# Spreading one-hot groups over the whole U stage, and loading a V group's tiles in four pieces between gathers

## What is computed

```python
def block(xb):                                   # for each token
    q = (xb @ w_q).reshape(p, HEADS, 2, 64)
    sc = einsum('phcd,hcnd->phcn', q, sub_keys)
    top_s, top_i = top_k(sc, 16)                 # of 128 keys, for both halves
    cand_s = top_s[..., 0, :, None] + top_s[..., 1, None, :]
    best_s, best_pos = top_k(cand_s, 16)         # 16 of 256 pairs
    idx = ...                                    # 8 heads * 16 of 16384 experts
    g = softmax(best_s)
    act = gelu(einsum('phkd,pd->phk', expert_u[idx], xb))
    return einsum('phk,phkd->pd', g * act, expert_v[idx])
```

## Time and profile before

| what | us |
|---|---|
| median of 3 runs | 2368.6 |
| the profiled execution | 2364.9 |
| its span | 2363.6 |
| PE busy | 2249.3 (95%) |
| DVE busy | 1616.6 (68%) |
| POOL busy | 1062.2 (45%) |
| ACT busy | 850.0 (36%) |

### The profile page before, as it was taken

How to read it: one execution, slowest core, us unless ns; L and a number is a source line. 1 busy time by engine, 2 the same in 40 slices (tenths; PEclk the granted TensorE clock), 3 DMA queues, 4 the chain that set the end, 5 groups by cost and what they waited for, 6 DMA issues and landing times.

```text
span 2363.6 us, 29994 instructions
## 1 busy us (share of the span) xinstructions
PE 2249.3 (95%) x11272; PEld 2031.7 (86%) x11272; DVE 1616.6 (68%) x3044; ACT 850.0 (36%) x1317; POOL 1062.2 (45%) x666
## 2 busy tenths in 40 slices
PE   6999999999889999899999989999999989999998
PEld 3777889998889999889899988998887778888887
DVE  6774699999996525878787878865756556444333
ACT  4433433333334333233333323354345533322221
POOL 1444207788888873545454645543332331111100
PEclk9999999999899999999999999999999999999999
DMA  7647747667668866999999999942424252333332
GB/s 291 196 139 248 218 126 183 171 154 172 151 150 201 210 169 202 338 367 353 374 343 368 338 366 331 347 152 85 122 74 118 74 178 89 102 95 98 103 98 76
DMA packets 205464, 470.89 MB, mean 199 GB/s; under 512 B 50364, under 2 KB 105788, under 8 KB 200768
## 3 DMA queue, kind: packets, MB, share of 16 engines
q1 hardware_dynamic: 136408, 316.76, 41.2%
q0 software_dynamic: 68912, 152.21, 21.0%
HBM read 403.68 MB, written 61.28 MB: 197 GB/s over the span
## 4 chain that ended last, share of the span: by engine, by line
PE 34%; DMA 11%; DVE 11%; POOL 3%; issue 2%; ACT 1%; DVEq 0%; ACTq 0%
PE bank L568 8%; PE bank L572 8%; PE bank L569 8%; DMA row_over<-in_rows_u,row_at 2%; DMA rows<-in_rows_v,row_at 2%; DVE own L2116 2%; DMA scaled<-in_rows_v,row_at 2%; DVE weights_lo L1654 2%; DMA square<-in_rows_u,row_at 2%; DMA rows<-in_rows_u,row_at 2%; DVE hidden L2077 1%; PE bank_stat L947 1%; PE bank_stat L948 1%; PE bank_stat L952 1%; DVE rows L2110 1%
## 5 line engine op out<-in xcount | busy, mean ns | idle before, releaser
L568 PE MATMUL bank<-h_lo,weights_hi 128*128 128x416 f32 (+1 forms) x2148 | 796.0, 371 | 10.2 <-DVE gates L2330 3.8
L569 PE MATMUL bank<-h_hi,weights_hi 128*128 128x416 f32 (+1 forms) x2148 | 791.1, 368 | 0.0
L1131 ACT ACTIVATE weights_hi<-weights_raw 128x1024 fp32r<-128x1024 f32 (+1 forms) x411 | 431.5, 1050 | 311.9 <-DMA weights_raw<-in_expert_v 176.8
L1654 DVE TENSOR_TENSOR weights_lo<-weights_raw,weights_hi 128x1024 fp32r<-128x1024 f32 x351 | 443.1, 1263 | 146.9 <-ACT weights_hi L1131 144.2
L2508 POOL DMA_INDIRECT expert_coefs<-square x256 | 444.3, 1735 | 157.7 <-issue 78.8
L572 PE MATMUL bank<-h_hi,weights_lo 128*128 128x416 f32 (+1 forms) x2148 | 482.8, 366 | 15.8 <-DVE weights_lo L1654 15.4
L568 PEld LDWEIGHTS bank<-h_lo,weights_hi 128*128 128x128 f32 x2148 | 411.1, 191 | 46.0 <-DVE gates L2330 3.9
L572 PEld LDWEIGHTS bank<-h_hi,weights_lo 128*128 128x128 f32 x2148 | 403.7, 189 | 51.5 <-DVE weights_lo L1654 21.2
L569 PEld LDWEIGHTS bank<-h_hi,weights_hi 128*128 128x128 f32 x2148 | 410.9, 191 | 30.7 <-issue 0.2
L2455 POOL TENSOR_TENSOR weights_lo<-weights_raw,weights_hi 128x1024 fp32r<-128x1024 f32 x60 | 147.9, 2471 | 220.6 <-ACT weights_hi L1131 220.6
L1342 ACT ACTIVATE hidden<-bank 128x416 f32<-128x416 f32 x128 | 66.2, 518 | 347.2 <-PE bank L572 331.6
(11 more groups left out here) (471 smaller groups left out, 3530.1 us busy)
## 6 DMA issues: line engine op xcount, KB each, us to landing
weights_raw<-in_expert_u SPq DMA_DIRECT2D x128, 512.0 KB
weights_raw<-in_expert_v SPq DMA_DIRECT2D x128, 512.0 KB
weight<-expert_coefs POOLq DMA_DIRECT2D x16, 1664.0 KB, 11.0
hidden_store<-hidden SPq DMA_DIRECT2D x28, 832.0 KB
hidden<-hidden_store POOLq DMA_DIRECT2D x14, 1664.0 KB, 15.8
ada_raw<-in_w_ada SPq DMA_DIRECT2D x34, 512.0 KB, 6.5
expert_coefs<-zeros SPq DMA_DIRECT2D x32, 512.0 KB, 6.4
weights_raw<-in_w_ffn_gate SPq DMA_DIRECT2D x22, 512.0 KB
```

The lines of the kernel that those rows point to most:

```text
L568: M.matmul(bank[:, 0:width], hi[:, c:c + P], m_lo[k][:, 0:width], start=start and i == 0, stop=False)
L569: M.matmul(bank[:, 0:width], hi[:, c:c + P], m_hi[k][:, 0:width], start=False, stop=False)
L1131: S.activation(w_hi[n % SPLIT][:, 0:w], w_raw[n % RAW][:, 0:w], ACT.Copy).then_inc(*hi_done.inc(n))
L1654: V.tensor_tensor(w_lo[n % SPLIT][:, 0:w], w_raw[n % RAW][:, 0:w], w_hi[n % SPLIT][:, 0:w].bitcast(F32), ALU.subtract).then_inc(*lo_dve.in ...
```

## The change

Two edits that don't depend on each other.

The first moves work inside the U stage. The routing steps of block 3 stand at every third step from j = 46 to j = 97, where they stood at every second from 46 to 80. The 32 quads of block 2 stand from j = 48 to 98 (before: one at each step from 48 to 79), and the 8 quads of block 3 from 100 to 112 (before: 83 to 97). The own tokens are copied at j = 113 (before: 98). No instruction is added or taken away.

The second cuts each `load_group` into four DMAs (two halves of the coefficients, two halves of the hidden values) and issues them after the gathers number 4, 6, 8 and 10 of the group, counted from 0, where both whole DMAs stood after gather 4. The wait for the hidden values of `mix_tile` becomes two: at tile 0 for the first half, at tile 4 for the second. The first two groups are loaded ahead of the gathers as before, in more pieces.

```diff
         for tb in range(1, TB):
-            step = 2 if tb == TB - 1 else 1
+            step = 3 if tb == TB - 1 else 1
             ROUTED_AT.append([ROUTED_AT[-1][-1] + 1 + step * n for n in range(ROUTE_STEPS)])
...
-            room = min(n_quads * TB // 2, QUADS, AHEAD * GROUP - 2 - first)
+            room = (ROUTED_AT[TB - 1][-1] + 3 if tb < TB - 1 else AHEAD * GROUP - 6) - first
...
                 if n == 0:
-                    V.wait_ge(*weight_landed[g % 2][g])
-                    if g < KEPT:
-                        V.wait_ge(*hidden_landed[g % 2][g])
+                    V.wait_ge(*weight_landed[g % 2][g, 1])
+                if n in (0, HALF) and g < KEPT:
+                    V.wait_ge(*hidden_landed[g % 2][g, n])
...
                     if i >= 2:
                         G.wait_ge(*dve["mix_lo", MIX_ORDER[i - 2], GROUP - 1])
-                    G.dma_start(weight[g % 2][:].rearrange("p s j t -> p (s j t)"),
-                                coefs[g].rearrange("p s j t -> p (s j t)")).then_inc(*weight_landed[g % 2].inc(g))
+                    half = DT // TOK // 2
+                    for part in range(2):
+                        yield G.dma_start(weight[g % 2][:, part * half:(part + 1) * half].rearrange("p s j t -> p (s j t)"),
+                                          coefs[g, :, part * half:(part + 1) * half].rearrange("p s j t -> p (s j t)")) \
+                            .then_inc(*weight_landed[g % 2].inc((g, part)))
                     if g < KEPT:
                         G.wait_ge(*hidden_stored[g % 2][g, HALF])
-                        G.dma_start(hidden[g % 2][:], hidden_store[g]).then_inc(*hidden_landed[g % 2].inc(g))
-
-            load_group(0)
+                        for n in (0, HALF):
+                            yield G.dma_start(hidden[g % 2][:, n:n + HALF, :], hidden_store[g, :, n:n + HALF, :]) \
+                                .then_inc(*hidden_landed[g % 2].inc((g, n)))
...
+                pieces = load_group(i + 2)
                 for n, q in enumerate(steps_here):
                     load_rows(q)
-                    if n == ROWS - 1:
-                        load_group(i + 2)
-                if len(steps_here) < ROWS:
-                    load_group(i + 2)
+                    if n >= ROWS - 1 and (n - ROWS + 1) % 2 == 0:
+                        next(pieces, None)
+                for _ in pieces:
+                    pass
```

More of the change, by code:

```diff
@@ L2520, in load_group @@
                         G.wait_ge(*dve["mix_lo", MIX_ORDER[i - 2], GROUP - 1])
-                    G.dma_start(weight[g % 2][:].rearrange("p s j t -> p (s j t)"),
-                                coefs[g].rearrange("p s j t -> p (s j t)")).then_inc(*weight_landed[g % 2].inc(g))
+                    half = DT // TOK // 2
[3 more added lines that the diff above has]
+                            .then_inc(*weight_landed[g % 2].inc((g, part)))
                     if g < KEPT:
                         G.wait_ge(*hidden_stored[g % 2][g, HALF])
-                        G.dma_start(hidden[g % 2][:], hidden_store[g]).then_inc(*hidden_landed[g % 2].inc(g))
-            load_group(0)
+                        for n in (0, HALF):
+                            yield G.dma_start(hidden[g % 2][:, n:n + HALF, :], hidden_store[g, :, n:n + HALF, :]) \
+                                .then_inc(*hidden_landed[g % 2].inc((g, n)))
+            for _ in load_group(0):
+                pass
             G.dma_start(position[:], a["positions"]).then_inc(*position_landed.inc("position"))
-            load_group(1)
+            for _ in load_group(1):
+                pass
             def load_rows(q):
```

## The result

The changed kernel takes 2302.3 us (median of four runs, 2296.5 to 2305.8) against 2368.6: a ratio of 0.9716, with an interval of 0.969 to 0.9741. It is 66 us faster; the forecast was 40. The profiled execution took 2305.8 us with a span of 2304.5, 59.1 us under the span of before. The part behind the last group, which no edit of this document touches, took 807.9 to 814.3 us in the fourteen traces: that is how much two executions differ there alone.

A forecast was written before the change was run, and what follows sets the result against it. VectorE was taken to bound the U stage's middle, TensorE its end, with GpSimd's scatters alongside, and VectorE with one late gather the V stage. 2364.9 - 2 - 38 = 2324.9 us, as a median 2328; range 2312 to 2360.

The forecast's parts named there:

- The U stage: U stage, first edit: TensorE sets the pace, so u119 comes about 30 us earlier, near 878 us.
- Where that gain goes: End of U stage: nowhere; TensorE stands still some 30 us because the first mixing waits for coefficients behind the last scatter.
- The hand-over's own shift: Scatters' end before the first mixing: -2 us taken, with -6 and +21 us kept as ends.
- The 2 us for calls beside an idle VectorE: Last 20 us or so of scatters: about 11 calls at 1.54 us rather than 1.735, 2 us less.
- The V stage: V stage, second edit: VectorE's stop for the late gather goes; 14 periods shorten by 2.7 us each, -38 us.
- the allowance for queueing: V stage: gathers and weight blocks queue now and then near the 418 GB/s ceiling, so 37.1 us a period (382 GB/s).
- the sign of being right: V stage in the profile after: the loads' spacing is 36.5 to 37.5 us.
- the best case: V stage: all 14 passes with a load fall from 39.8 to 35.8 us, -56 us.
- 8.5 against 13.0: V stage: a gather behind a piece lands in 8.5 us, where five buffers in flight allow 13.0 us.
- the two favourable ends: The scatters' end at -6 us and the V stage's gain at -56 us.
- The rule against small DMAs: Skill's rule of DMAs of at least 1 MiB: 30 more would cost an estimated 60 us in series; expected to cost little.
- the wrong one of these two rules: Scatters: the skill's inference that two-input instructions don't lock GpSimd out would make the -2 us term 0.

The follow-up runs named there:

- the two cut kernels: The last 32 of 256 scatters left out: the changed kernel so cut took 2281.1 us (0.9649), the kernel before so cut 2359.9 us (0.9977).
- the run that fills the pause by order: Changed kernel with the splits and gelus of u120 to u127 put ahead of group 14's mixing on VectorE and ScalarE: 2307.7 us, 0.9751.
- the run with the cut-down chain: Changed kernel with table steps done before the coefficients, seven row steps spread over the V stage, mixing in pairs beside the last four splits: 2282.7 us, 0.9644.

## Why the prediction came out short

Its mechanisms held in the main, and two terms of its sum were too small.

- **The U stage.** Right: u119 at 878.45 us (forecast: near 878, with 4 us allowed for small stalls; that it fits to the microsecond is luck), steps of 4.5 to 5.0 us nearly throughout, the clock at 1.00.
- **Where that gain goes.** Right: a pause up to the first mixing. That it hangs on the scatters is shown by the two cut kernels. The pause costs clock (0.79 and 0.88 in the two stretches, 0.70 from 905 to 915 us), and mostly under the cover of VectorE's chain, as was said: the chain of waits runs through VectorE and the one gather from 904.2 to 941.6 us. Not covered is a second dip behind the stop at 939 us: the last eight matmuls of group 14's first product take 3.14 us (944.04) where they take 1.67 at the full clock (922.42, above).
- **The hand-over's own shift: -2 us taken, 8 to 9 measured.** This is the first mis-sized term. The last scatter ended 5.8 us earlier, where -6 had been named as the end of the range and -2 taken. The 2 us for calls beside an idle VectorE were right (30.2 us for 32.5); what failed is the step that left the calls ahead of these at their old mean, though quads now run beside them; the 20 just before gained 0.5 to 5 us. And one part was missed: the coefficients land 6.8 us after GpSimd begins to issue them (897.41 to 904.2), where it had been 9.1. In those 9.1 us the DMA queues also moved 0.52 MB of other data, a block of weights; in the 6.8 us none. The second edit alone (6.9, none) and the run that fills the pause by order (8.5, 0.53 MB) fit this, so it goes with the weight loads and not with TensorE's pause as such; the first edit alone, whose load is whole, takes 7.3 with none. The chain of waits has the last 6.2 of these, from the issue of the second piece:

```profile
898.02 6.17 DMA weight<-expert_coefs
```

- **The V stage: -38 us taken, 51 to 52 measured.** The second and larger one. VectorE's waits for gathers fell from 103 us to 23 (forecast: under 30) and TensorE is what is late next, as written. The step that failed is the allowance for queueing: 37.1 us a period was taken for a data rate near its ceiling, and TensorE came through without a gap. From the load of pass 0 to that of pass 13 a period fell from 39.9 to 36.0 us, which is TensorE's own pace and less than the 36.5 to 37.5 named as the sign of being right; from u127 to the last group 51.7 us were saved, of the 56 named as the best case. The rate could follow: 390 GB/s at a share of 0.99. Queueing did come, as the longer gathers show, but VectorE's four small waits per 100 us vanish under its own slack of 50 us in 476, and so cost nothing.
- **A number right for a wrong reason.** A gather behind a piece was put at 8.5 us, from one with an empty queue. At 382 GB/s and with five buffers it takes 12.0 (the run with the cut-down chain), and four buffers (10.1 us) are too few. The argument "8.5 against 13.0" gave the right answer with far less room than it claimed.
- **The range.** 2312 was above the sum of the two favourable ends: 2368.6 - 6 - 56 = 2306.6. Both ends had been worked out, and both were close to what came; the range took one part of each. That sum lies inside the measured interval (0.969 to 0.9741 of 2368.6 is 2295 to 2307), so the 4 us between it and 2302.3 can't be told from the spread of the executions.
- **The rule against small DMAs.** The Trainium skill's fixed cost of about 2 us a DMA (DMA: Bandwidth & Descriptors, the anatomy of a DMA) didn't show where the DMA engines are busy 0.99 of the time: the runs with 30 more DMAs are the faster ones, and four pieces beat two.

## What to carry to other kernels

Where two chains end within 10 us of each other, shortening one of them alone gives next to nothing: of the 30 us won in the U stage 8 came through, and those because the scatters and the load behind them became shorter too. Leaving out a part of the other chain (here, 32 scatters) shows what stands behind it. A large load in the same queue as small urgent ones delays whoever is next, here by 12 us for 3328 KB; cut it up between them, and check that buffers times pace still exceed the latency at the data rate that will then hold. Work that an engine does behind a late arrival, but which doesn't need it, belongs ahead of it: moving table steps and row steps away from the first mixing gave 20 us, where filling the other engine's pause by order alone gave none.

## What the runs showed of the hardware

An indirect DMA issued by GpSimd (1.54 us) is held up if a two-input subtraction of VectorE on SBUF operands is already running when it begins, and then by what is left of that less 0.12 us, up to 0.83 us of 0.95. A subtraction that begins during the call doesn't hold it, nor is it held: the 21 that did took 1.22 to 1.23 us like the others. In the stretches looked at (58 calls) no other instruction of VectorE was running when a call began, so they don't tell whether others do the same.

A plain load issued by GpSimd isn't held. In the traces of the kernels before and after, 25 of them begin while such a subtraction is running, with up to 0.98 us of it ahead, and take 0.58 to 0.61 us as always; one of the kernel before:

```profile
1156.80 0.61 POOL L2525 DMA_DIRECT2D hidden<-hidden_store  x1
...
1156.50 1.22 DVE L1654 TENSOR_TENSOR weights_lo<-weights_raw,weights_hi 128x1024 fp32r<-128x1024 f32 x1
```

The scatter differs from the load in that it takes its row numbers and its values from SBUF. The Trainium skill (SBUF — State Buffer, "Who interferes with whom") says that a VectorE instruction with two SBUF inputs contends with a GpSimd instruction that reads SBUF; the held scatters agree with that. Its inference that the two-input form doesn't stop descriptor writing agrees with the loads, as far as the length of an issue shows it. So the prediction set the wrong one of these two rules against its term. The Trainium skill (SBUF — State Buffer, "SBUF: two separate sides") also calls this a lock held for the whole instruction, in which whoever comes second is blocked: the rows show that for a scatter behind a subtraction, and not the other way round.

The two can fall into step, as before the change, where a step of 4.48 us holds exactly one call of 2.33 and one of 1.54 with their 0.30 us gaps (2.33 + 0.30 + 1.54 + 0.30 = 4.47): every second call then pays.
